# The weight ring of a two-block fp32 model moved 64 bytes along SBUF, everything behind the constants 128 bytes

## The reference

```
h = rms_norm(x, norm_g);  proj = h @ w_in                # 1024 -> 11 thousand columns
ys = stack([y_a, y_b, y_c, y_d])                         # each 256 x 512
branch_d = einsum('nbsw,nwd->bsnd', ys, w_branch)
out = x + sum(sigmoid(gates) * branch_d) @ w_out
```

## Time and profile before

| | |
|---|---|
| median of 3 runs | 1172.37 us (1170.7 to 1172.52) |
| span of the profiled execution, first to last instruction | 1167.6 us |
| the median less that span | 4.8 us |
| TensorE busy | 1019.9 us, 87% |
| VectorE, ScalarE, GpSimd busy | 506.4, 380.4, 427.5 us |
| DMA | 304.75 MB, mean 261 GB/s |
| mean granted TensorE clock | 0.945 |

### The profile page before, as it was taken

The page is one execution under the profiler, slowest core; times in us unless marked ns, Lnnn a source line. Parts: engine busy times, 40 slices in busy tenths (PEclk is TensorE's granted clock), DMA queues, the critical chain, the costliest instruction groups (busy, mean ns, idle before and its releaser), DMA issues.

```text
span 1167.6 us, 20205 instructions
## 1 busy us (share of the span) xinstructions
PE 1019.9 (87%) x8173; PEld 802.9 (69%) x8173; DVE 506.4 (43%) x980; ACT 380.4 (33%) x572; POOL 427.5 (37%) x192
## 2 busy tenths in 40 slices
PE   8999999999999999999999899966767667666685
PEld 6999999999999999797989797423323232332231
DVE  4346965601136887767854543222222222222213
ACT  5554354444447656334343344100000000000002
POOL 6767868888876866143031281000000000000000
PEclk9999999999999999999999899988888888888898
DMA  7644546566656544215220889999999999999995
GB/s 248 219 129 146 178 129 187 175 192 186 183 178 196 165 146 137 59 37 217 93 80 12 326 293 383 388 425 428 429 427 428 429 427 429 428 428 429 428 420 202
DMA packets 43569, 304.75 MB, mean 261 GB/s; under 512 B 5092, under 2 KB 5476, under 8 KB 30952
## 3 DMA queue, kind: packets, MB, share of 16 engines
q1 hardware_dynamic: 43208, 303.21, 69.1%
q10 hardware_dynamic: 288, 0.52, 0.1%
HBM read 302.67 MB, written 1.05 MB: 260 GB/s over the span
## 4 chain that ended last, share of the span: by engine, by line
PE 57%; DMA 27%; DVE 8%; POOL 2%; issue 2%; ACT 2%; SPq 2%; DVEq 0%; ACTq 0%; POOLq 0%
DMA arena<-gate_up 24%; PE bank L484 11%; PE bank L485 11%; PE bank L486 10%; PE bank L1357 6%; PE bank L862 5%; PE bank L1378 3%; POOL rounded L2966 1%; DMA weights<-front 1%; DMA arena<-down 1%; PE bank L826 1%; DVE arena L2091 1%; POOL rounded L2925 1%; SPq L3010 1%; PE bank L1097 1%
## 5 line engine op out<-in xcount | busy, mean ns | idle before, releaser
L2925 POOL TENSOR_TENSOR rounded<-weights,rounded 128x1024 fp32r<-128x1024 f32 x152 | 370.4, 2463 | 156.3 <-ACT rounded L1443 146.9
L484 PE MATMUL bank<-rounded 128*128 128x256 f32 (+2 forms) x776 | 219.2, 282 | 2.2 <-POOL rounded L2925 2.2
L485 PE MATMUL bank<-rounded 128*128 128x256 f32 (+2 forms) x776 | 216.5, 279 | 0.0
L486 PE MATMUL bank<-rounded 128*128 128x256 f32 (+2 forms) x776 | 216.2, 279 | 0.0
L1443 ACT ACTIVATE rounded<-weights 128x1024 fp32r<-128x1024 f32 x146 | 147.4, 1052 | 80.6 <-PE bank L486 47.6
L484 PE MATMUL bank<-rounded,rounded 128*128 128x256 f32 (+3 forms) x552 | 158.3, 287 | 2.1 <-DVEq L2346 0.8
L485 PE MATMUL bank<-rounded,rounded 128*128 128x256 f32 (+3 forms) x552 | 156.2, 283 | 0.0
L486 PE MATMUL bank<-rounded,rounded 128*128 128x256 f32 (+3 forms) x552 | 156.1, 283 | 0.0
L484 PEld LDWEIGHTS bank<-rounded 128*128 128x128 f32 (+1 forms) x776 | 145.6, 188 | 4.3 <-POOL rounded L2925 2.9
L485 PEld LDWEIGHTS bank<-rounded 128*128 128x128 f32 (+1 forms) x776 | 145.5, 187 | 0.7 <-issue 0.6
L486 PEld LDWEIGHTS bank<-rounded 128*128 128x128 f32 (+1 forms) x776 | 145.2, 187 | 0.0
(11 more groups left out here) (465 smaller groups left out, 1456.6 us busy)
## 6 DMA issues: line engine op xcount, KB each, us to landing
weights<-front SPq DMA_DIRECT2D x165, 512.0 KB, 4.2
arena<-down SPq DMA_DIRECT2D x31, 2048.0 KB, 22.0
weights<-gate_up SPq DMA_DIRECT2D x28, 2048.0 KB, 34.7
arena<-gate_up SPq DMA_DIRECT2D x28, 2048.0 KB, 33.4
weights<-front SPq DMA_DIRECT2D x4, 2048.0 KB, 8.0
weights<-gate_up SPq DMA_DIRECT2D x8, 768.0 KB, 12.5
arena<-gate_up SPq DMA_DIRECT2D x4, 1536.0 KB, 33.7
weights<-gate_up SPq DMA_DIRECT2D x4, 512.0 KB, 7.3
```

Source lines behind the costliest of these rows:

```text
L484: nc.tensor.matmul(out, a[0], b[1], start=start, stop=False)
L485: nc.tensor.matmul(out, a[0], b[0], start=False, stop=False)
L486: return nc.tensor.matmul(out, a[1], b[0], start=False, stop=stop)
L2925: nc.gpsimd.tensor_tensor(lo, raw[q % RAW], hi.bitcast(f32), ALU.subtract).then_inc(sem("w_lo"), 1)
```

## The change

Sixteen columns (64 bytes) that nothing uses are put ahead of the ring, and the arena is made 16 columns shorter, so that its end stays where it was. `layer_base` is rounded up to a multiple of 32 columns in place of 8, which takes it from 3728 to 3744. In bytes of a partition: the ring, `res` and the constants move by 64; all that is laid out from `layer_base` moves by 128 and so keeps its place modulo 128; `odd` and the down buffers stay where they were. Afterwards the ring's buffers and `h1` both lie 64 bytes off a multiple of 128. No instruction, shape, wait or order changes.

```diff
-        RING, ARENA = SLOTS * BLOCK, 40664
-        with nc.sbuf_tensor("weights", [P, RING], f32) as weights, nc.sbuf_tensor("arena", [P, ARENA], f32) as arena:
+        FIRST, RING, ARENA = 16, SLOTS * BLOCK, 40648
+        with (nc.sbuf_tensor("ahead", [P, FIRST], f32), nc.sbuf_tensor("weights", [P, RING], f32) as weights,
+              nc.sbuf_tensor("arena", [P, ARENA], f32) as arena):
             pass
...
-            if at == 0:
-                with nc.sbuf_tensor(f"rounded_{name}", [P, cols], f32r) as x:
-                    return x[:, :]
-            with nc.sbuf_tensor(f"below_{name}", [P, at], f32), nc.sbuf_tensor(f"rounded_{name}", [P, cols], f32r) as x:
+            with nc.sbuf_tensor(f"below_{name}", [P, FIRST + at], f32), nc.sbuf_tensor(f"rounded_{name}", [P, cols], f32r) as x:
                 pass
...
-        top[0] = layer_base = -(-top[0] // 8) * 8
+        top[0] = layer_base = -(-top[0] // 32) * 32
```

## The result

The changed kernel takes 1174.95 us, median of 20 runs (1171.94 to 1179.3), against 1171.37 (20 runs, 1168.75 to 1174.58) of the kernel before. The ratio is 1.0033, 95% interval 1.0022 to 1.0043: slower, by some 3.6 us where 6.7 were forecast. The profiled execution spans 1173.2 us. Lines from 127 on are two less than before: L482 to L484 are `matmul3`, L2923 GpSimd's subtraction.

A forecast was written before the change was run, and what follows sets the result against it. TensorE's product pitch was taken to bound the first block, loading the experts. First block after cover 6.4, `wf` -0.1 and parts +0.4 summed to +6.7 us: 1179.1 us, range 1173 to 1183.

The forecast's parts named there:

- What bounds the kernel, and where a change of places can act: TensorE paces 250 to 300 us, loading the experts; places act through product pitch before about 700 us or load rate after.
- That the relation of the two places sets the pitch: TensorE products: operands at the same place modulo 128 cost 120.0 ns, differing by 64 they cost 113.3 or 117.9.
- No conflict: Rival, chance 0.11: 120.0 ns belongs to set 4 for another reason, and time stays at 1172.4, within 2.3 us.
- After the change every product of the first block, and every part, is in the position of set 4.: First block and parts: all products take set 4's 120.0 ns, from 113.3 or 117.9 before.
- weaker witness: `wf` products, both operands at multiples of 128: 118.6 ns each, taken as the low bound of the new pitch.
- the first block's term: First block: 432 products lose 6.7 ns and 2232 lose 2.1 ns, together 7.6 us before cover.
- its low case: First block at pitch 118.6: 3.9 us lost, less 2.2 of cover, giving about 1174.1 us.
- Cover: First block, 98 to 164 us: slower TensorE shortens its wait behind VectorE's chain; 1.2 us taken off, at most 2.2.
- Other engines and DMAs at nothing: GpSimd's splits, the loads, `res` and the constants: the 64-byte offset priced at zero.
- Parts: Parts near the end, 13 of 16 in the ring: 0.4 us lost, between 0 and 1.0, with GpSimd's splits setting time.
- `wf` a little faster: Second block: `wf` operands become unequal; 4 x 24 products gain at most 0.5 us, likelier 0.1.
- Faster: Rival, chance 0.09: the short pitch holds everywhere, 2232 products gain 10.3 us, some 9 after the VectorE stretch: 1163 us.

The follow-up runs named there:

- ring alone: Changed kernel without the new rounding of `layer_base` (3728), so only the ring moves by 64 bytes: 1172.54 us, ratio 1.0002 to the kernel before.
- activations alone: Kernel before with only the new rounding of `layer_base` to 32 columns, the ring unmoved: 1174.72 us, ratio 1.0032.
- the second small kernel: Standalone kernel without the model, high and low operands 8192 bytes apart, 20 placements, 8 runs of 48 products each: 113.3 to 120.0 ns a product.
- distance 0: Changed kernel with `layer_base` at 3776 in place of 3744, first-block activations and ring equal modulo 256 bytes: 1178.99 us, ratio 1.0076.
- the small kernels: Standalone kernels without the model, running 48-product stretches at chosen operand places; the last walks distances 0 to 248 in steps of 8 bytes.
- distances 192, 32 and 112: Kernel before with first-block activations 192, 32 or 112 bytes from the ring modulo 256: 1172.2, 1170.61, 1165.58 us (112 with the second block moved too: 1165.98).

## Why the prediction was right or wrong

*What bounds the kernel, and where a change of places can act*: right. The loss is in the first block's pitch; the rate of the loads is the same.

*That the relation of the two places sets the pitch*: right (ring alone 1.0002, activations alone 1.0032). *No conflict* falls by the same two runs. The Trainium skill, "SBUF — State Buffer", section "SBUF: two separate sides", has TensorE wait for nobody. The page speaks of engines among each other, and no run here contradicts that; but the reading that a place then costs nothing is contradicted by the second small kernel, 113.3 to 120.0 ns by nothing but places.

*The step that failed* is "After the change every product of the first block, and every part, is in the position of set 4." It holds modulo 128. In the runs the distance counts modulo 256, where set 4 has distance 0 and the changed first block 128. The rows told it, had each place been worked out to more bits: the equal places at 120.0 were all distance 0, the "weaker witness" at 118.6 was distance 128 and was the exact likeness of what the change makes. So 120.0 was taken where 118.6 was right for most products; the mean came to 118.85, and the first block's term to 4.5 us in place of 7.6. The prediction's own sign of being wrong, stretches near 118 ns in the first block, is what the timeline shows from 216.83 us. The measured time lies inside the range 1173 to 1183 because its low case, 1174.1, was worked out from the 118.6 ns of `wf`: the rule of modulo 128 was wrong, but that row, kept as a bound, was the right price for most products. With the first block really in set 4's position the time was 1178.99 us. That the sum of 1179.1 meets it is in part luck, since a part of that kernel's loss lay outside the first block.

*Cover*: 1.2 us was taken off, 0.9 is what pitch sum and delay differ by in one pair of traces (0.8 at distance 0). *Other engines and DMAs at nothing*: as shown above. *Parts*: 0.4 forecast; the delay grows by 0.7 from 660 to 713 us in the profiled execution. *`wf` a little faster*: not seen, since its first 2.5 us ran at the lower clock.

*Faster*, "if the new places let the short pitch hold everywhere": not at distance 128. Such a place exists, 112, and there 2590 products less 2.8 ns are 7.3 us, of which 3.5 are left at the end of the block and 5.4 in the medians; the difference between these two isn't resolved.

*The mechanism*, next weights and moving stream meeting in one half of a 128-byte line, was marked as an inference, and doesn't stand in that form: the span is 256 bytes, and distance 96 costs as much as 0. The Trainium skill, "TensorE: Matmul & The Clock Gate", section "Step-by-step: what each phase is for", says that loading the next weights takes no read bandwidth from the running product. A pitch that hangs on the distance between the two operands is hard to bring together with that, but no run took the weight loads away, so which two accesses meet stays open. Also open is what picks 113.3 or 117.8 at distances 64 and 192.

## What to carry to other kernels

Where TensorE is full and one shape shows several pitches, work out the distance between its moving and its stationary operand modulo 256 bytes, and match prices only between rows of the same distance: here the list ran from 113.3 to 122.7 ns for the same product. A short pitch can then be chosen by moving one buffer (112 bytes: 0.9955), but only where TensorE alone sets the pace is the gain sure. A faster TensorE also brings forward the work that waits for it: here a split on GpSimd came to start 0.2 to 0.8 us ahead of a cast on VectorE, and cast, wait and clock took back some 3.5 us. So before a gain is booked, look in the trace for what the faster engine releases and what that will run beside. A price seen at one place is worth a small kernel that walks through the places before it goes into a sum.

## What the runs showed of the hardware

- The pitch of a 256-column product in the rounded format follows the distance of its operands modulo 256 bytes, with the weights at 0 or at 64 and in the model as in the small kernels: 0 gives 120.0 ns, 32 116.7, 64 and 192 113.3 or 117.8, 128 118.6 (some runs 120.0), 8 mostly 122.7 on average over 48 products. Distance 144 is an exception: 116.7 to 118.9 in the small kernel, 120.0 in the model.
- At distance 112 the first ten or so products of a run take about 117 ns, all others 113.3, in 5 of 5 runs and in the model.
- At some distances there are two or three steady values, and a run takes another after a few float32 products: at 64 each of the small kernel's runs stays at 113.3 or at 117.8.
- In the first block a cast of 128x512 on VectorE takes 0.43 us when it starts outside a split on GpSimd and 1.5 to 2.5 us when it starts inside one, in all ten traces of the model.
- Behind a wait of TensorE of 3.1 to 3.2 us in the first block the granted clock was 0.93 from 140 to 165 us, at distances 192, 32 and 112; with a wait of 0.7 us at the same place, in the kernel before, it stayed at 1.00.
